# New orders at nine turns between the stages of a two-block network, and the first mixer's first units in token halves

## The reference

```python
def first_block(x, p, ...):
    z = rms_norm(h, norm_mix_g)
    proj = z @ w_in                                   # 1024 x 1536: pool, lru, gate
    y_pool = multiscale_pool_mixer(u_pool, ...)       # window means 2, 4, 8, 16 and a 128 x 128 product each
    xb = causal_depthwise_conv(u_lru, conv_w, conv_b)
    y_lru = rg_lru(xb, ...) * gelu(u_gate)            # two gate products, sigmoid, linear recurrence
    h = h + concatenate([y_pool, y_lru]) @ w_out
    h = h + square(relu(rms_norm(h) @ w_up)) @ w_down # mlp, 4096 wide
    h = h + sigmoid(rms_norm(h) @ w_ple_gate + b) * (p @ w_ple_proj)
    return rms_norm(h, norm_final_g)

def second_block(x, ...):
    x = x + 0.5 * rms_norm(swiglu(rms_norm(x), w_in, w_out))     # ffn1, 2816 wide
    q, k, v, u = split(rms_norm(x) @ w_mix_in, 4)
    attn = dilated_attention(q, k, v)                 # 8 heads, three dilations, ALiBi
    ssm = s5_mixer(u, ...)                            # diagonal SSM, then a GLU with w_glu
    x = x + rms_norm(concatenate([attn, ssm]) @ w_mix_out)
    return x + 0.5 * rms_norm(swiglu(rms_norm(x), ...))          # ffn2
```

## Time and profile before

| | us |
|---|---|
| median of 3 runs | 3071.19 (3071.16 to 3071.35) |
| the profiled execution | 3068.12 |
| its span | 3066.3 |
| PE busy | 3012.4 (98%) |
| DVE busy | 1356.8 (44%) |
| ACT busy | 869.9 (28%) |
| POOL busy | 408.9 (13%) |

### The profile page before, as it was taken

How to read it: one execution, slowest core, us unless ns; L and a number is a source line. 1 busy time by engine, 2 the same in 40 slices (tenths; PEclk the granted TensorE clock), 3 DMA queues, 4 the chain that set the end, 5 groups by cost and what they waited for, 6 DMA issues and landing times.

```text
span 3066.3 us, 36769 instructions
## 1 busy us (share of the span) xinstructions
PE 3012.4 (98%) x14144; PEld 2470.2 (81%) x14144; DVE 1356.8 (44%) x1763; ACT 869.9 (28%) x1324; POOL 408.9 (13%) x1004
## 2 busy tenths in 40 slices
PE   7999999999999999999999999999899999999998
PEld 6777888888888878888888878876688888888887
DVE  5664444444445453333333362346646333333335
ACT  6523221122114352111111143146644111111112
POOL 0000000000000001988850010012100000000000
PEclk9999999999999999999999999999999999999999
DMA  3121111111112121223221132212132111111113
GB/s 128 41 87 65 62 48 35 54 55 55 36 47 64 47 83 49 74 95 109 85 73 41 48 144 69 77 65 94 48 119 80 55 49 48 52 58 41 41 48 130
DMA packets 54409, 206.98 MB, mean 68 GB/s; under 512 B 7216, under 2 KB 7984, under 8 KB 52000
## 3 DMA queue, kind: packets, MB, share of 16 engines
q1 hardware_dynamic: 38592, 140.53, 13.8%
q0 software_dynamic: 15712, 65.02, 5.8%
HBM read 173.15 MB, written 31.20 MB: 67 GB/s over the span
## 4 chain that ended last, share of the span: by engine, by line
PE 93%; DVE 4%; ACT 2%; issue 1%; DMA 0%; SPq 0%; DVEq 0%; ACTq 0%
PE ps L126 29%; PE ps L127 29%; PE ps L128 29%; PE ps L262 1%; PE ps L1887 1%; PE ps L1913 1%; PE ps L1928 1%; DVE sco L1901 0%; DVE acc L177 0%; DVE acc L185 0%; ACT junk L198 0%; DVE scx L510 0%; PE ps L1563 0%; ACT junk L164 0%; PE ps L321 0%
## 5 line engine op out<-in xcount | busy, mean ns | idle before, releaser
L126 PE MATMUL ps<-region_a,region_b 128*128 128x512 f32 x1664 | 655.9, 394 | 11.1 <-DVE region_a L221 7.3
L128 PE MATMUL ps<-region_a,region_b 128*128 128x512 f32 x1664 | 648.6, 390 | 0.0
L127 PE MATMUL ps<-region_a,region_b 128*128 128x512 f32 x1664 | 648.3, 390 | 0.0
L126 PE MATMUL ps<-region_b,region_a 128*128 128x512 f32 x1088 | 428.3, 394 | 1.9 <-DVE region_b L121 1.9
L128 PE MATMUL ps<-region_b,region_a 128*128 128x512 f32 x1088 | 424.8, 390 | 0.0
L127 PE MATMUL ps<-region_b,region_a 128*128 128x512 f32 x1088 | 424.6, 390 | 0.0
L900 DVE TENSOR_TENSOR acc<-acc,ps 128x1024 f32<-128x1024 f32 x240 | 293.0, 1221 | 293.6 <-PE ps L128 293.6
L121 DVE TENSOR_TENSOR region_b<-raw,region_b 128x1024 fp32r<-128x1024 f32 x176 | 216.1, 1243 | 369.0 <-ACT region_b L117 368.5
L126 PEld LDWEIGHTS ps<-region_a,region_b 128*128 128x128 f32 x1664 | 313.0, 188 | 78.4 <-issue 8.5
L128 PEld LDWEIGHTS ps<-region_a,region_b 128*128 128x128 f32 x1664 | 312.8, 188 | 65.5
L127 PEld LDWEIGHTS ps<-region_a,region_b 128*128 128x128 f32 x1664 | 313.2, 188 | 64.4 <-issue 1.7
(11 more groups left out here) (291 smaller groups left out, 3252.7 us busy)
## 6 DMA issues: line engine op xcount, KB each, us to landing
raw<-stream SPq DMA_DIRECT2D x252, 512.0 KB, 3.3
ssm_row<-ssm_mid POOLq DMA_DIRECT2D x8, 1632.0 KB, 7.6
x_mid<-acc POOLq DMA_DIRECT2D x24, 512.0 KB, 2.9
ssm_mid<-made_osc POOLq DMA_DIRECT2D x8, 1024.0 KB, 4.3
ssm_mid<-made_out POOLq DMA_DIRECT2D x8, 608.0 KB, 3.6
acc<-x SPq DMA_DIRECT2D x8, 512.0 KB, 8.0
rold<-x POOLq DMA_DIRECT2D x16, 256.0 KB, 3.6
old_a<-x_mid POOLq DMA_DIRECT2D x8, 512.0 KB, 8.7
```

The lines of the kernel that those rows point to most:

```text
L126: nc.tensor.matmul(psum, lhs(0), rhs(0), start=first, stop=False)
L127: nc.tensor.matmul(psum, lhs(0), rhs(1), start=False, stop=False)
L128: return nc.tensor.matmul(psum, lhs(1), rhs(0), start=False, stop=last)
```

## The change

Nothing that is computed changes. These orders do:

- First mixer: the transpositions no longer all stand ahead of the products; products of units 0 and 1 follow two steps behind (`front`). The first four units are lru 0 and gates 0 to 2, first their first halves, then their second. Gate values go straight into the output tile Y. Gate and pool products stand behind other groups.
- w_out to mlp: the eight steps of the first half each stand one place earlier; so do those of the second half.
- Gated first chunk: six banks for its eight groups where it had four.
- ffn1 to the second mixer: transposition steps stand at other places of the last products; second half of the norm in groups 3 and 4 of Q and K.
- V: the four units of U are split behind the second and fourth copy of V.
- End of attention: the quotient of a pair stands ahead of the last maximum, values ahead of the SSM step, and two weight units are split later on DVE.
- Output product to ffn2: pieces of the split are grouped otherwise.

The core of the diff (`F.gated` holds for ffn1 and ffn2, not for the mlp):

```diff
@@ -26,6 +26,8 @@
 SSM_ROW = 4 * 512 + 2 * 576 + 64
 
 
+UNITS1 = [("lru", 0), ("gate", 0), ("gate", 1), ("gate", 2), ("lru", 1), ("lru", 2), ("pool", 3), ("lru", 3),
+          ("pool", 2), ("gate", 3), ("pool", 1), ("pool", 0)]
...
@@ -275,10 +277,14 @@
 
 
         n_first = Norm("g_mix", A, lambda t: (x_in[t], 16))
-        UNITS1 = [(kind, j) for j in range(4) for kind in ("lru", "gate")] + [("pool", j) for j in (3, 2, 1, 0)]
         TALL1 = len(UNITS1)
-
-        GROUPS1 = [(0, 0), (1, 0), (0, 1), (1, 1)] + [(m, half) for m in range(2, TALL1) for half in range(2)]
+        FRONT1 = 4
+        GROUPS1 = [(m, half) for half in range(2) for m in range(FRONT1)] + \
+                  [(m, half) for m in range(FRONT1, TALL1) for half in range(2)]
+        GATES_BEHIND = {6: 0, 10: 1, 14: 2, 18: 3}
+        POOL_BEHIND = {16: 0, 19: 1, 22: 2}
+        SMALL1 = [("gate", n) for n in range(12)] + [("pool", n) for n in range(2)] + \
+                 [("gate", n) for n in range(12, 16)] + [("pool", n) for n in range(2, 8)]
...
+
+            def front(k):
+
+                for m in range(2):
                     pe.wait_ge(unit_ready, m + 1)
-                for g in (2 * m, 2 * m + 1):
-                    mm, half = GROUPS1[g]
-                    if g < 2:
-                        pe.wait_ge(unit_ready, mm + 1)
-                        pe.wait_ge(*n_first.at("lo", 8))
-                    if g == 2:
-                        norm_pe_step(pe, n_first, 1, 7)
-                        pe.wait_ge(*n_first.at("lo", 16))
-                    if g >= 4:
-                        pe.wait_ge(*out_of(*GROUPS1[g - 4]))
-                    each = (lambda k: norm_pe_step(pe, n_first, 1, k)) if g == 1 else None
-                    tall_group(pe, A, B[:, mm % 4], KD, half, g % 4, each).then_inc(in_done, 1)
-                    if g == 2 * TALL1 - 2:
-                        poolmm(pe, 2)
-                if m == 2:
+                    last = products(ps[:, m, :], lambda h: B[:, m, h, k * P:(k + 1) * P],
+                                    lambda h: A[:, k, h, 0:HALF], k == 0, k == KD - 1)
+                    if k == KD - 1:
+                        last.then_inc(in_done, 1)
+
+            for d in range(KD):
+                norm_pe_step(pe, n_first, 0, d)
+                if d >= 2:
+                    front(d - 2)
+            for k in (KD - 2, KD - 1):
+                pe.wait_ge(*n_first.at("lo", k + 1))
+                front(k)
+            for g in range(2, 2 * TALL1):
+                m, half = GROUPS1[g]
+                pe.wait_ge(unit_ready, m + 1)
+                each = None
+                if g < 4:
+                    def each(k, at=8 * (g - 2) - late):
+                        if 0 <= at + k < KD:
+                            norm_pe_step(pe, n_first, 1, at + k)
+                if g == 3:
+                    norm_pe(pe, n_first, 1, 7 - late, 8 - late)
+                if g == 4:
+                    pe.wait_ge(*n_first.at("lo", 16))
+                if g >= 4:
+                    pe.wait_ge(*out_of(*GROUPS1[g - 4]))
+                tall_group(pe, A, B[:, m % 4], KD, half, g % 4, each).then_inc(in_done, 1)
+                if g == 6:
                     pe.wait_ge(mats_in, 48)
-                if m % 2 == 0 and 2 <= m <= 8:
-                    gates(pe, m // 2 - 1)
-                if m == 9 or m == 10:
-                    poolmm(pe, m - 9)
+                if g in GATES_BEHIND:
+                    gates(pe, GATES_BEHIND[g])
+                if g in POOL_BEHIND:
+                    poolmm(pe, POOL_BEHIND[g])
...
-            split_act(act, n_first, 0)
-            for m in range(2, 4):
-                hi1(act, m)
-            norm_act(act, n_first, 1)
+            split_act(act, n_first, 0, range(3))
+            for t in range(4, NT):
+                pre_act(act, n_first, t)
+                if t < NT - 1:
+                    split_act(act, n_first, 0, (t - 1,))
+            split_act(act, n_first, 0, (6,))
+            hi1(act, 2)
+            split_act(act, n_first, 0, (7,))
+            hi1(act, 3)
+            evac1(act, 0)
+            split_act(act, n_first, 1)
 
...
@@ -448,10 +487,12 @@
             dve.wait_ge(params_in, 16)
             for m in range(2):
                 make_lo(dve, m, B[:, m % 4], m % 2)
-            split_dve(dve, n_first, 0)
-            for m in range(2, 4):
-                make_lo(dve, m, B[:, m % 4], m % 2)
-            norm_dve(dve, n_first, 1)
+            split_dve(dve, n_first, 0, range(7))
+            make_lo(dve, 2, B[:, 2], 0)
+            split_dve(dve, n_first, 0, (7,))
+            norm_dve_rows(dve, n_first, 1)
+            make_lo(dve, 3, B[:, 3], 1)
+            split_dve(dve, n_first, 1)
...
+            convolve(0)
+            for m in (4, 5, 6):
+                lo1(m)
+            recur(0)
+            lo1(7)
+            convolve(1)
...
@@ -602,10 +651,12 @@
                 pe.wait_ge(W.evac_of, g - banks + 1)
                 for i in range(KD):
                     last = part(half, t, i, i == 0, i == KD - 1)
+                    if g == NT + 5 and i == 7:
+                        norm_pe_step(pe, norm, 0, 0)
                     if g == NT + 6 and i % 2:
-                        norm_pe_step(pe, norm, 0, i // 2)
-                    if g == NT + 7 and i % 2 == 0:
-                        norm_pe_step(pe, norm, 0, 4 + i // 2)
+                        norm_pe_step(pe, norm, 0, 1 + i // 2)
+                    if g == NT + 7 and i in (0, 2, 4):
+                        norm_pe_step(pe, norm, 0, 5 + i // 2)
...
@@ -706,7 +757,7 @@
         def up_bank(F, c, j, half):
 
             if F.gated and at_start(c):
-                return (j + 2) % 4
+                return ((2, 3, 0, 1), (4, 5, 2, 3))[half][j]
             return 2 * j + half if by_halves(F, c, j) else half
...
@@ -731,11 +782,9 @@
                 pe.wait_ge(unit_ready, F.n_up(c, j) + 1)
                 if halves and g in F.banks:
                     pe.wait_ge(*F.banks[g])
-                if F.gated and isinstance(c, int) and c == 1 and g == 0:
-                    pe.wait_ge(*F.at("ge", 2 * CHUNK))
                 if F.gated and halves:
-                    if half:
-                        pe.wait_ge(*F.at("sq" if j % 2 else "ge", f + 1))
+                    if g in (6, 7):
+                        pe.wait_ge(*F.at("sq" if j % 2 else "ge", 1))
...
+                if norm and not F.gated and g == 0:
+                    each = lambda k: norm_pe_step(pe, norm, 1, 0) if k == 6 else None
                 if norm and not F.gated and g == 1:
-                    each = lambda k: norm_pe_step(pe, norm, 1, k)
-                if norm and not F.gated and g == 2:
-                    norm_pe(pe, norm, 1, 7)
+                    each = lambda k: norm_pe_step(pe, norm, 1, k + 1)
                 if norm and g == (4 if F.gated else 2):
                     pe.wait_ge(*norm.at("lo", 16))
...
@@ -1215,11 +1264,14 @@
                 if n == 2:
                     pe.wait_ge(*ffn1.at("de", f1_all))
                 if n == 4:
-                    norm_pe_step(pe, n_mix2, 1, 7)
                     pe.wait_ge(*n_mix2.at("lo", 16))
                 if n >= 4:
                     pe.wait_ge(qk_out, n - 3)
-                each = (lambda k: norm_pe_step(pe, n_mix2, 1, k)) if n == 3 else None
+                each = None
+                if n in (2, 3):
+                    def each(k, at=-5 if n == 2 else 2):
+                        if 0 <= at + k < KD:
+                            norm_pe_step(pe, n_mix2, 1, at + k)
                 tall_group(pe, A, B[:, SLOTS4[m % 4]], KD, half, n % 4, each).then_inc(qk_done, 1)
...
@@ -1275,8 +1327,9 @@
             for t in range(NT):
                 dve.wait_ge(v_done, t + 1)
                 nc.vector.tensor_copy(V[:, t, :], ps[:, V_BANKS[t % 4], :]).then_inc(v_out, 1)
-                if t % 2:
-                    lo_of(dve, u_unit(t // 2))
+                if t == 1 or t == 3:
+                    lo_of(dve, u_unit(t - 1))
+                    lo_of(dve, u_unit(t))
...
@@ -1943,8 +1997,10 @@
                 transposes(n)
                 if n == 0:
                     ssm_turn_pe(pe, 0, 0)
+                if n == NA - 1:
+                    values(m - 1, True)
                 ssm_step_pe(pe, n)
-                if m:
+                if m and n < NA - 1:
                     values(m - 1, n % 2 == 1)
...
@@ -2004,25 +2060,25 @@
 
             made = {}
             for n in range(NA):
-                if n % 2 == 0 and n >= 4:
+                if n % 2 == 0 and 4 <= n < NA - 2:
                     finish(n // 2 - 2)
+                if n == NA - 3:
+                    finish(NA // 2 - 3)
                 if n + 2 < NA:
...
                     made[h + 2] = head_bias(dve, h + 2)
-                if n == NA - 4:
-                    lo_of(dve, front_unit())
                 ssm_step_dve(dve, n)
                 if n % 2 == 0 and n:
```

(26 more changed lines are left out.)

121 lines of the change are left out of this document (65 added, 56 removed).

## The result

The changed kernel takes 3049.69 us (median of 4, 3048.02 to 3051.37), the kernel before 3071.27 beside it; the ratio is 0.9932, 95% interval 0.9919 to 0.9944. The forecast was 3053.7 (3049.5 to 3062): the measured median is inside the range by only 0.2, and outside the forecast's own range of 3050.5 to 3057.5. The medians differ by 21.6. The forecast did not see why the two differ. The profile of before was from the faster executions of its kernel, the profile after from the slower ones of its own: its four took 3048.0, 3048.2, 3051.2 and 3051.4.

The account below looks back on a forecast made before the run. TensorE, 98% busy, bounds the kernel, so only its idle 43.8 us can yield time. Terms sum to 17.5: 3068.12 profiled becomes 3050.6, or 3053.7 as median; 8-in-10 range 3049.5 to 3062, own range 3050.5 to 3057.5.

Parts of the forecast that it names:

- a: Start of the kernel, first mixer: products among transpositions start earlier and the clock rises earlier; gain 7.5 us, bounds 3.7 to 8.5.
- Rivals 1 and 4: First mixer: lacing makes the clock rise late (3058.8 us, chance 0.15), or keeps it low, so slower (3077.4, chance 0.03).
- b: w_out to mlp: earlier splits and transposition steps close or shorten two gaps; gain 1.8 us.
- c: First chunk of ffn1: six banks remove the wait for an unemptied bank, the last split still holds; gain 1.2 us.
- f: V to U: units split earlier, so the stop before the first U product goes; gain 2.3 us.
- d: ffn1 to second mixer: a step moved behind 12 products, which run in the gap; gain 1.1 us.
- e: Second half of Q and K: a 1.56 us gap goes, a new one of 1.2 comes; gain 0.5 us.
- g: Tail of attention: quotient and values earlier, output product starts earlier; nominal 3.75 us, taken as 3.2, bounds 1.9 and 3.9.
- h: Output product to ffn2: a 0.71 us gap goes but later splits give it back; net -0.1 us, bounds -0.6 and 0.7.
- The carry to the median: Whole kernel: the profiled execution lay 3.1 us below the median, so forecast 3050.6 profiled became 3053.7 as median.

Follow-up runs that it names:

- d_undone: Changed kernel with the transposition steps of the second mixer's norm back at their old places in ffn1's last products; median 3050.60 or 3050.84 us (text leaves open which).
- a_nolace: Changed kernel with all 32 transpositions of the first half ahead of the first product again; no total time given, fifth group 8.7 us later than in the changed kernel.
- bcf_undone: Changed kernel with w_out to mlp, the banks of ffn1's first chunk and the splits of U's units in old order; 3057.61 us, ratio 0.9962.
- after_filld: Changed kernel with seven matmuls nobody reads in the 1.88 us wait for an emptied bank at 1804.5; median 3048.83 us, ratio 0.9934.
- best_b: Changed kernel with second-mixer norm steps moved, ffn2's old split, three unread matmuls in attention's tail, earlier mlp transpositions and norm splits; 3047.64 us, ratio 0.9931.
- g_undone: Changed kernel with the tail of attention in its old order; 3055.43 us, ratio 0.9953.

## Why the prediction was right, point by point

- **a** held in its mechanism: products at 15.17 (15.6), level up at 20.01 (20.0), fifth group at 45.3 (45.6). 0.3 more are waits late in the mixer that went, another 0.3 the earlier load of x. That the rise met its time to the hundredth is luck: in the nine profiles with laced products the granted clock went to 1.00 between 18.37 and 20.26. Counted from the first transposition, the latest rise goes with a gain of 7.8 (the changed kernel) and the earliest with 9.0 (d_undone). Rivals 1 and 4, with the lacing holding the clock down, are out: the level rose with transpositions among the products. ACT does bound the steps without the lacing (a_nolace, 1.94 a step); the prediction had named this as up to 1.0 and left it out of the sum, which did not need it.
- **b, c, f** held to 0.1 (1.9, 1.1 and 2.3 against 1.8, 1.2 and 2.3), and all three go when they are undone together (bcf_undone): waits whose releaser had nothing behind it but what the next row showed.
- **d is the step that failed.** The text let 12 products "run in the gap". Nine of them did: the shift rose from 11.3 to 14.2. But the step was then behind tile 7's wait for a bank, which L1018 empties, and on DVE that stands behind the row that the transposition itself needs: 1.88 of new wait, one of the things to ask of a moved step that I asked only of the later additions.

```profile
1802.60 0.75 DVE L210 TENSOR_SCALAR xn<-acc,small 128x1024 f32<-128x1024 f32 x1
1803.26 1.21 DVE L1018 TENSOR_TENSOR acc<-acc,ps 128x1024 f32<-128x1024 f32 x1
```

The first transposition, at 1805.34, came 1.95 later than the shift ahead of the turn would have put it, and the chain behind moved with it. Without the clock's fall the turn is worth 0.3 (after_filld) and not 1.1; with it -1.3. **e** gave 0.5 as forecast, but it depends on d: 1.2 in d_undone, where d gave -0.4, and -0.9 in best_b, where d gave 2.2. Together d and e were forecast at 1.6 with 0.6 as the lower bound, and gave -0.8; without the fall 0.8.
- **g** gave 4.3, above its upper bound of 3.9. The 3.75 nominal was for a tail without a fall against one with it, and the 3.2 allowed in part for a fall that comes again. Measured: 4.2 to 4.3 in the profiles without a fall, 2.7 and 2.8 with one, and 2.1 in d_undone with a fall and a late load of the GLU weights, close to the 1.9 that the prediction gave for just that. Which of them a profile shows is chance, and here it was the best. The mechanism stands (g_undone).
- **h** held in sign (-0.3), and the old order there is better.
- **The carry to the median failed in size.** Profile for profile the sum of 17.5 met 16.9, in part by luck: the fall that came in d (1.6 lost) stood nowhere in the sum, and g (1.1 over its term, with no fall) and a (0.6 over, 0.3 of it the load of x) made up for it. And I added the constant 3.1 between the profiled execution and the median of before as if it belonged to every execution. It comes from two heaps: the profile of before was of the lower one, its median of the upper. Two of the changed kernel's four executions lie at 3048.1 and two at 3051.3, its profile among the latter, so its median of 3049.69 is a midpoint. From before's upper heap to the midpoint is 21.6, from its profile to the slower pair 16.9. Of the 3.2 between the changed kernel's pairs, its fall at 1805.42 explains 1.6; the rest is not shown.

## What to carry to other kernels

Before a median and a profile of a kernel are set against each other, look at the granted clock behind every gap: a kernel that is 98% busy still lost 0.4 to 1.6 us at each of four, in some executions only, and a change that closes gaps can win those too. When a step is moved past others on an engine that runs in order, ask of each thing it is moved past what that waits for, the bank that it writes included. And where a gain of 1 to 2 us is smaller than the spread, read it as a shift of the same numbered instruction in two profiles with the same clock, not from medians.
